# Rotary score products over all 128 rows instead of 64, with the upper rows zeroed by GpSimd

## The chip, the cores and the metric

The kernel runs on one core of a Trainium2 chip. The metric is the time of one execution on the device in microseconds (us), and the time of a kernel is the median of its runs. Five engines share the core: TensorE (PE in the profile, its weight loads PEld), VectorE (DVE), ScalarE (ACT), GpSimd (POOL) and SyncE (SP). Each runs its own list of instructions in order, and they wait for one another on semaphores.

## The reference

The reference is a stack of four layers for 256 tokens of width 2048: two of one family, then two (`l` = 0, 1) of another. The change lies in the latent attention of the last two. Each of 8 heads has queries and keys of 192 numbers: 128 plain ones, and 64 that are turned by the position (the rotary part). Scores are the dot product of all 192, so they are the sum of a product over 128 and one over 64.

```python
def mla_mixer(q_a, kv_a, k_rope, cos, sin, q_a_norm_g, w_q_b, kv_a_norm_g, w_kv_b, q_norm_g, k_norm_g):
    ...
    k_pe = jnp.broadcast_to(k_rope[:, :, None, :], (bsz, seq, MLA_HEADS, MLA_ROPE))
    k = jnp.concatenate([k_nope, k_pe], axis=-1)
    q = rms_norm(q, q_norm_g)
    k = rms_norm(k, k_norm_g)
    q = jnp.concatenate([q[..., :MLA_NOPE], apply_rope(q[..., MLA_NOPE:], cos, sin)], axis=-1)
    k = jnp.concatenate([k[..., :MLA_NOPE], apply_rope(k[..., MLA_NOPE:], cos, sin)], axis=-1)
    o = causal_block_attention(q, k, v, MLA_QK_HEAD ** -0.5)

def causal_block_attention(q, k, v, scale):
    for blk in range(seq // Q_BLOCK):            # Q_BLOCK = 128, so two blocks
        q0 = blk * Q_BLOCK
        kend = q0 + Q_BLOCK
        s = jnp.einsum('bqhd,bkhd->bhqk', q[:, q0:kend], k[:, :kend]).astype(jnp.float32) * scale
        mask = (q0 + jnp.arange(Q_BLOCK))[:, None] >= jnp.arange(kend)[None, :]
        p = jax.nn.softmax(jnp.where(mask, s, -jnp.inf), axis=-1)
        outs.append(jnp.einsum('bhqk,bkhd->bqhd', p.astype(v.dtype), v[:, :kend]))
```

The attention's output goes, beside that of a state-space mixer, through a projection (`w_out`), and the layer goes on with a cross attention and a feed-forward part.

## The kernel before

Nearly all the time goes into large products with weights. The weights come from memory in pieces of 128 x 2048 numbers. SP issues the transfers; ACT splits a piece into a high part (`w_hi`, L451, which waits until TensorE has done with the piece three earlier, `SETS = 3`); DVE computes the low part (`w_lo`, L459); and TensorE multiplies high by high, low by high and high by low (L531 to L533, L539 to L541, L547 and L549).

The small work of a layer, attention among it, is hung between these pieces. `layer_at(eng, l, idx, step)` puts a step on an engine's list behind piece `idx` of the layer. Each engine builds its list in the order of the pieces, so what stands in a list is fixed when the program is written, and only the semaphores decide when it runs.

The attention of layer `l` has eleven steps on TensorE, `step(0)` to `step(10)`, behind the pieces 34 to 44. In step `s` stand

- `load(s)`: eight transposes of head `s` (L1359 and L1360) into the scratch banks `M`; the last adds one to `la_turned`. ACT copies the 128 plain rows to `la["qk"]`, and DVE copies the 64 rotary rows to the lower half of `la["qkr"]` (L2199). There are two such buffers of 128 partitions x 512 numbers, for even and odd heads.
- `att_scores_pe` of head `s - 1`: for each of the two blocks of queries the plain product (L1030), the rotary product (L1032) and an addition of the causal mask as a product with the identity in bf16 (L1034). The first block takes 128 keys, the second 256. An fp32 product is two instructions in the profile.
- the product with the values of head `s - 3` (L1101, L1103) and the turn of head `s - 2`'s probabilities (L1088).

The maximum, the exponential and the scaling of a head's scores run on DVE (L1042, L1046, L1062, L1065) and ACT (L1055) meanwhile, and the turn in the next step waits for them.

GpSimd has little to do. Its list issues the small transfers. Around the change these are the gains of layer `l` (`mla_gains`), issued when the layer's first piece has started, and then, once both halves of the state-space output are ready (`ssd_out` at 2l + 2), the two parts of the transposed memory (`memT`) for the cross attention. The upper halves of `la["qkr"]` lie where temporaries of the rotation stood earlier (`la["rt"]`).

Of the kernel before, what the change touches and what calls it, by code (L numbers as in the profile page):

```python
# [28 lines left out]
P = 128  # L29
D = 2048  # L30
T = 256
# [102 lines left out]
def build(nc, dram, out_ap):  # L134
    ctx = ExitStack()
    with ctx:
# [5 lines left out]
        def S(name):  # L142
            if name not in sems:
                sems[name] = ctx.enter_context(nc.semaphore(name))
            return sems[name]
# [117 lines left out]
        la = dict(kr=Area(2048)(2, 8, 64), q=a(2, 8, 192), k=a(2, 8, P), v=a(2, 8, P))  # L263
# [517 lines left out]
        def n(eng, name, k=1):  # L781

            key = (eng.engine, name)
            tallies[key] = tallies.get(key, 0) + k
            return tallies[key]
# [238 lines left out]
        def att_scores_pe(pe, h, q, k, causal, rope=None):  # L1024
            pe.wait_ge(S("q_k_ready"), n(pe, "q_k_ready"))
            bank = M[:, 2 + h % 2, :]
            for t, (c0, w) in enumerate(cuts(causal)):
                tok = slice(t * P, t * P + P)
                o = bank[:, c0:c0 + w]
                mm = pe.matmul(o, q(h)[:, tok], k(h)[:, 0:w], start=(t == 0), stop=not causal, skip_group_check=True)  # L1030
                if rope:
                    pe.matmul(o, rope(h)[0][:, tok], rope(h)[1][:, 0:w], start=False, stop=False, skip_group_check=True)  # L1032
                if causal:
                    mm = pe.matmul(bank[:, c0 + w - P:c0 + w], identb[:, :], mask_ts[:, :], start=False, stop=True,  # L1034
                                   skip_group_check=True)
            mm.then_inc(S("att_scores"), 1)
# [48 lines left out]
        def att_turn_pe(pe, h, p, causal, l):  # L1085
            pe.wait_ge(S("att_probs"), n(pe, "att_probs"))
            for _, _, c, ct in blocks(causal):
                mm = pe.transpose(turn_bank(h, causal, l)[:, ct:ct + P], p[h % 2][:, c:c + P], ident[:, :])  # L1088
            mm.then_inc(S("att_turned"), 1)
# [6 lines left out]
        def att_values_pe(pe, h, pt, v, causal, l):  # L1096
            pe.wait_ge(S("att_pt"), n(pe, "att_pt"))
            if causal and h:
                pe.wait_ge(S("att_out"), n(pe, "att_out"))
            o = value_bank(h, causal, l)[:, 0:T]  # L1100
            pe.matmul(o, v(h, 0), pt[h % 2][:, 0:T], start=True, stop=False, skip_group_check=True)  # L1101
            if causal:
                mm = pe.matmul(o[:, P:T], v(h, 1), pt[h % 2][:, T:T + P], start=False, stop=True, skip_group_check=True)  # L1103
            else:
                mm = pe.matmul(o, v(h, 1), pt[h % 2][:, T:2 * T], start=False, stop=True, skip_group_check=True)
            mm.then_inc(S("att_values"), 1)
# [10 lines left out]
        def att_close_pe(pe, m):  # L1117

            pe.wait_ge(S("att_out"), n(pe, "att_out", m))
# [136 lines left out]
        def layer_at(eng, l, idx, step):  # L1256

            at_piece(eng, first_piece[f"ssd{l}"] + idx, step)
# [93 lines left out]
        def mla_pe(pe, l):  # L1352
            def load(h):
                if h:
                    pe.wait_ge(S("la_loaded"), n(pe, "la_loaded", 2))
                for j, (a, r) in enumerate(((la["q"][:, :, :, 0:P], la["q"][:, :, :, P:192]), (la["k"], la["kr"]))):
                    for t in range(NT):
                        c = j * T + t * P
                        pe.transpose(M[:, 0, c:c + P], a[:, t, h, :], ident[:, :])  # L1359
                        mm = pe.transpose(M[0:64, 1, c:c + P], r[:, t, h, :], ident[:, :])  # L1360
                mm.then_inc(S("la_turned"), 1)

            q = lambda h: la["qk"][h % 2][:, 0:T]
            k = lambda h: la["qk"][h % 2][:, T:2 * T]
            rope = lambda h: (la["qkr"][h % 2][0:64, 0:T], la["qkr"][h % 2][0:64, T:2 * T])
            v = lambda h, s: la["v"][:, s, h, :]

            def step(s):
                if s == 0:
                    pe.wait_ge(S("la_ready"), l + 1)  # L1370
                    pe.wait_ge(S("la_k"), l + 1)
                    pe.wait_ge(S("sd_exp"), 16 * l + 16)
                if s < 8:
                    load(s)
                if 0 <= s - 1 < 8:
                    if s - 1 < 2:
                        pe.wait_ge(S("z_root"), 2 * l + s)
                    att_scores_pe(pe, s - 1, q, k, True, rope)
                if 0 <= s - 3 < 8:
                    att_values_pe(pe, s - 3, la["pt"], v, True, l)  # L1380
                if 0 <= s - 2 < 8:
                    if s == 2:
                        c = plans[f"va{l}"][1]
                        pe.wait_ge(S(f"set_free{c.slot}"), c.c // 2 + 1)
                    att_turn_pe(pe, s - 2, la["p"], True, l)

            def close():
                att_close_pe(pe, 1)
                pe.wait_ge(S("la_loaded"), n(pe, "la_loaded", 2))

            for s in range(11):
                layer_at(pe, l, 34 + s, lambda s=s: step(s))
            layer_at(pe, l, 46, close)
# [887 lines left out]
        @block.sync  # L2281
        def _(sp):
            sp_stream(sp)
# [5 lines left out]
        @block.gpsimd  # L2289
        def _(pool):  # L2290

            def load(o, i, s):
                pool.dma_start(o, i).then_inc(S(s), 16)

            load(par[:], dram["params"], "first_const")
            load(ident[:], dram["ident"], "first_const")
            for o, nm in ((identb, "identb"), (mask_st, "mask_st"),
                          (mask_ts, "mask_ts"), (select, "head_select"), (level, "level"), (invf, "inv_freq"), (posi, "positions")):
                load(o[:], dram[nm], "const")
            load(cbias[:, 0:8], dram["c_b_i"][0].partition_broadcast(P), "const")  # L2300
            load(cbias[:, 8:16], dram["c_b_f"][0].partition_broadcast(P), "const")
            for v, nm in ((dt_b, "dt_bias_2"), (al_b, "a_log_2")):
                load(v, dram[nm].partition_broadcast(P), "const")
            load(ple_in[:], dram["pT"][0].rearrange("(k p) t -> p k t", p=P), "p_loaded")

            pool.wait_ge(S("piece_done"), started("lru", 3))
            for g, nm in enumerate(("b_w_r", "b_w_i")):
                load(lr["w"][:, g], dram[nm][0].rearrange("n c d -> c n d"), "gate_w")

            pool.wait_ge(S("lru_lo"), 1)  # L2310
            load(res[:], dram["x"].rearrange("b (t p) d -> p (b t) d", p=P), "res_back")

            pool.wait_ge(S("piece_done"), started("e_out_a", 1))
            load(pe_["gain"], dram["ple_norm"][0].partition_broadcast(P), "gain_loaded")
            load(mem_tokens, dram["mem_2"].rearrange("b (t p) d -> p (b t) d", p=P), "mem_tokens")
            load(ple_in[:], dram["pT"][1].rearrange("(k p) t -> p k t", p=P), "p_loaded")

            pool.wait_ge(S("piece_done"), started("o_out", 3))
            load(pe_["gain"], dram["ple_norm"][1].partition_broadcast(P), "gain_loaded")
            load(fin["gain"], dram["final_norm"].partition_broadcast(P), "final_gain")  # L2320
            for l in range(2):
                pool.wait_ge(S("piece_done"), started(f"ssd{l}"))
                load(mlag[:, 0, :], dram["mla_q_norm_g_2"][l].partition_broadcast(P), "mla_gain")
                load(mlag[:, 1, :], dram["mla_k_norm_g_2"][l].partition_broadcast(P), "mla_gain")

                pool.wait_ge(S("ssd_out"), 2 * l + 2)
                for j in range(2):
                    load(mem_parts[j], dram["memT"][:, 8 * j:8 * j + 8, :], "mem_loaded")
            for j, c in enumerate(plans["down12"]):
                pool.wait_ge(S(f"set_free{c.c % 2}"), c.c // 2 + 1)  # L2330
                cols = slice(512 * j, 512 * j + 512)
                pool.dma_start(out_ap[:, :, cols].rearrange("b (t p) d -> p (b t) d", p=P), res[:, :, cols]
                               ).then_inc(S("stored"), 16)
            pool.wait_ge(S("stored"), 64)
# [352 lines left out]
```

## Time and profile before

| | us |
|---|---|
| median of 3 runs | 3562.82 |
| lowest and highest run | 3557.84, 3564.38 |
| profiled execution, its own time | 3560.18 |
| its span, first to last instruction | 3558.4 |
| TensorE busy | 3479.6 |
| VectorE busy | 2106.5 |
| ScalarE busy | 1720.2 |
| GpSimd busy | 20.8 |

The span is 1.8 us shorter than the execution's own time; the rest lies before the first and behind the last instruction. A row that begins with a time is a place in the span. "Busy" of TensorE counts an instruction from its start to its modelled end, and these intervals overlap, so what a product really takes is read from the distance between two starts. In a form such as `64*128 64x256` the first pair is rows and columns of the array in use, the second the operand.

### The profile page before, as it was taken

To read this page: it belongs to the slowest core of one execution; us is meant where nothing else is said; L and a number is where in the kernel's file an instruction comes from. 1 tells how busy PE (TensorE), PEld (TensorE's weight loads), DVE (VectorE), ACT (ScalarE), POOL (GpSimd) and SP (SyncE) were. 2 spreads that over 40 slices of the span, in tenths; PEclk is the share of its full clock that TensorE was granted. 3 is DMA by queue.
4 is the path that set the end of the run, shared out by engine and by line. 5 is a ranking of instruction groups with operands and counts; after the bars stand their busy time and mean duration, and the time that the engine had idled before them with its cause. 6 is when DMAs were issued, how large, how long until landed. Compare 5 with 4: busy or idle time off the path is not lost.

```text
span 3558.4 us, 43532 instructions
## 1 busy us (share of the span) xinstructions
PE 3479.6 (98%) x18590; PEld 2974.1 (84%) x18590; DVE 2106.5 (59%) x2186; ACT 1720.2 (48%) x2040; POOL 20.8 (1%) x38
## 2 busy tenths in 40 slices
PE   7999999999999999999999999999999999999999
PEld 6888888878778888888888888888888888888887
DVE  6766667544556866646555545577656555455454
ACT  4643464356545465555434434455745644344343
POOL 1000000000000000000000000000000000000000
PEclk9999999999999999999999999999999999999999
DMA  6554554544555444445555555554444455555554
GB/s 241 185 178 142 192 190 167 195 171 170 187 176 180 173 142 154 146 147 181 189 189 190 189 192 190 191 181 166 142 141 168 149 189 190 194 189 189 189 189 166
DMA packets 88578, 630.91 MB, mean 177 GB/s; under 512 B 10064, under 2 KB 10304, under 8 KB 13248
## 3 DMA queue, kind: packets, MB, share of 16 engines
q1 hardware_dynamic: 85104, 611.75, 49.5%
q0 software_dynamic: 3280, 16.36, 1.3%
q8 instruction: 147, 2.41, 0.3%
q14 instruction: 47, 0.39, 0.0%
HBM read 625.98 MB, written 2.10 MB: 177 GB/s over the span
## 4 chain that ended last, share of the span: by engine, by line
PE 86%; DVE 7%; ACT 5%; issue 1%; DMA 1%; DVEq 0%; POOL 0%; ACTq 0%; POOLq 0%
PE G L547 26%; PE G L539 13%; PE G L549 13%; PE G L541 13%; PE G L540 13%; DVE w_lo L459 3%; ACT w_hi L451 2%; PE G L531 1%; PE G L533 1%; PE G L532 1%; PE M L811 1%; PE M L1139 1%; DMA w_raw<-in_s_lru 1%; DVE arena L758 0%; PE M L1032 0%
## 5 line engine op out<-in xcount | busy, mean ns | idle before, releaser
L459 DVE TENSOR_TENSOR w_lo<-w_raw,w_hi 128x2048 fp32r<-128x2048 f32 (+1 forms) x585 | 1328.3, 2272 | 1253.5 <-ACT w_hi L451 1253.1
L451 ACT ACTIVATE w_hi<-w_raw 128x2048 fp32r<-128x2048 f32 (+1 forms) x585 | 1110.8, 1899 | 1608.3 <-PE G L549 744.6
L547 PE MATMUL G<-x_halves,w_hi 128*128 128x512 f32 x4256 | 1346.3, 397 | 20.5 <-DVE w_lo L459 15.4
L549 PEld LDWEIGHTS G<-x_halves,w_lo 128*128 128x128 f32 x4256 | 800.9, 188 | 188.5
L549 PE MATMUL G<-x_halves,w_lo 128*128 128x256 f32 x4256 | 841.2, 278 | 0.0
L547 PEld LDWEIGHTS G<-x_halves,w_hi 128*128 128x128 f32 x4256 | 651.6, 189 | 24.9 <-issue 14.7
L539 PE MATMUL G<-w_hi,y_halves 128*128 128x512 f32 x1648 | 648.8, 394 | 3.0 <-DVE y_halves L1114 2.6
L541 PE MATMUL G<-w_hi,y_halves 128*128 128x512 f32 x1648 | 642.1, 390 | 0.0
L540 PE MATMUL G<-w_lo,y_halves 128*128 128x512 f32 x1648 | 642.0, 390 | 0.0
L539 PEld LDWEIGHTS G<-w_hi,y_halves 128*128 128x128 f32 x1648 | 309.7, 188 | 67.9 <-DVE y_halves L1114 4.4
L541 PEld LDWEIGHTS G<-w_hi,y_halves 128*128 128x128 f32 x1648 | 309.6, 188 | 65.3
L540 PEld LDWEIGHTS G<-w_lo,y_halves 128*128 128x128 f32 x1648 | 309.8, 188 | 62.6
L539 PE MATMUL G<-w_hi,x_halves 128*128 128x512 f32 x448 | 176.7, 394 | 0.0
L541 PE MATMUL G<-w_hi,x_halves 128*128 128x512 f32 x448 | 175.1, 391 | 0.0
L540 PE MATMUL G<-w_lo,x_halves 128*128 128x512 f32 x448 | 175.1, 391 | 0.0
L547 PE MATMUL G<-y_halves,w_hi 128*128 128x512 f32 (+1 forms) x400 | 127.1, 398 | 0.0
L681 DVE TENSOR_TENSOR arena<-G,other_half 128x512 f32<-128x512 f32 (+1 forms) x143 | 97.2, 679 | 9.9 <-ACT other_half L604 9.3
L541 PEld LDWEIGHTS G<-w_hi,x_halves 128*128 128x128 f32 x448 | 84.5, 189 | 17.9
L539 PEld LDWEIGHTS G<-w_hi,x_halves 128*128 128x128 f32 x448 | 84.6, 189 | 17.0
L540 PEld LDWEIGHTS G<-w_lo,x_halves 128*128 128x128 f32 x448 | 84.5, 189 | 17.0
L549 PEld LDWEIGHTS G<-y_halves,w_lo 128*128 128x128 f32 (+1 forms) x400 | 73.6, 184 | 17.4
L604 ACT ACTIVATE other_half<-G 128x512 f32<-128x512 f32 (+1 forms) x147 | 84.5, 575 | 1.2 <-ACT ple_in L1668 0.8
(442 smaller groups left out, 2703.9 us busy)
## 6 DMA issues: line engine op xcount, KB each, us to landing
w_raw<-in_s_up SPq DMA_DIRECT2D x176, 1024.0 KB, 4.8
w_raw<-in_s_down SPq DMA_DIRECT2D x88, 1024.0 KB, 4.8
w_raw<-in_s_ssd SPq DMA_DIRECT2D x40, 1024.0 KB, 4.8
w_raw<-in_s_hgrn SPq DMA_DIRECT2D x32, 1024.0 KB, 4.8
w_raw<-in_s_gate SPq DMA_DIRECT2D x32, 1024.0 KB, 4.8
w_raw<-in_s_mlstm SPq DMA_DIRECT2D x32, 1024.0 KB, 4.8
w_raw<-in_s_mlstm_gate SPq DMA_DIRECT2D x32, 1024.0 KB, 4.8
w_raw<-in_s_lru SPq DMA_DIRECT2D x16, 1024.0 KB, 4.9
```

Of the source, the lines that this page charges most:

```text
L451: act.activation(whi[p % SETS][:, 0:n_], raw[p % RAW][:, 0:n_], ACT.Copy).then_inc(S("hi_ready"), 1)
L459: dve.tensor_tensor(wlo[p % SETS][:, 0:n_], raw[p % RAW][:, 0:n_], whi[p % SETS][:, 0:n_].bitcast(F32), ALU.subtract).then_inc(S("lo_ready ...
L531: pe.matmul(o, ah[:, kk, tok], hi[:, k, :], start=first and t == 0, stop=False, **kw)
L532: pe.matmul(o, ah[:, kk, tok], lo[:, k, :], start=False, stop=False, **kw)
L533: mm = pe.matmul(o, al[:, kk, tok], hi[:, k, :], start=False, stop=last, **kw)
L539: pe.matmul(o, ah[:, kk, tok], hi[:, k, :], start=first, stop=False)
L540: pe.matmul(o, ah[:, kk, tok], lo[:, k, :], start=False, stop=False)
L541: mm = pe.matmul(o, al[:, kk, tok], hi[:, k, :], start=False, stop=last)
L547: pe.matmul(o, hi[:, k, f], x2, start=first, stop=False, skip_group_check=True)
L549: mm = pe.matmul(o[:, 0:T], lo[:, k, f], x2[:, 0:T], start=False, stop=last, skip_group_check=True)
L604: act.activation(other_half[0:np_, 0:nb, :], bank_set(c)[0:np_, 0:nb, T:2 * T], ACT.Copy).then_inc(S("half_out"), 1)
L681: dve.tensor_tensor(dst, bank_set(c)[0:np_, 0:nb, 0:T], other_half[0:np_, 0:nb, :], ALU.add).then_inc(S(f"set_free{c.c % 2}"), 1)
```

## The change

Both operands of the rotary product are now read over all 128 partitions instead of the lower 64. To make the added rows add nothing, GpSimd writes zeros to the partitions 64 to 127 of both buffers, once in each layer. It waits for the first head's transposes of that layer (`la_turned` at 8l + 1), and TensorE waits for it (`rope_padded`) in step 1, ahead of the first scores.

```diff
-            rope = lambda h: (la["qkr"][h % 2][0:64, 0:T], la["qkr"][h % 2][0:64, T:2 * T])
+            rope = lambda h: (la["qkr"][h % 2][:, 0:T], la["qkr"][h % 2][:, T:2 * T])
...
                 if s < 8:
                     load(s)
+                if s == 1:
+                    pe.wait_ge(S("rope_padded"), l + 1)
                 if 0 <= s - 1 < 8:
...
                 load(mlag[:, 1, :], dram["mla_k_norm_g_2"][l].partition_broadcast(P), "mla_gain")
+
+                pool.wait_ge(S("la_turned"), 8 * l + 1)
+                for v in la["qkr"]:
+                    ins = pool.memset(v[64:P, :], 0.0)
+                ins.then_inc(S("rope_padded"), 1)
 
                 pool.wait_ge(S("ssd_out"), 2 * l + 2)
```

On GpSimd, in the part of its list for one layer, there stood before the change these rows, where the two transfers of `memT` follow the gains directly:

```order
28 L2293 DMA mla_gains<-in_mla_q_norm_g 128x192 [waits piece_done]
29 L2293 DMA mla_gains<-in_mla_k_norm_g 128x192
30 L2293 DMA arena<-in_memT 128x2048 [waits ssd_out]
31 L2293 DMA arena<-in_memT 128x2048
32 L2293 DMA mla_gains<-in_mla_q_norm_g 128x192 [waits piece_done]
```

Now two memsets of `la["qkr"]` (part of the `arena`) stand between them:

```order
28 L2295 DMA mla_gains<-in_mla_q_norm_g 128x192 [waits piece_done]
29 L2295 DMA mla_gains<-in_mla_k_norm_g 128x192
30 L2330 MEMSET arena 64x512 [waits la_turned]
31 L2330 MEMSET arena 64x512
32 L2295 DMA arena<-in_memT 128x2048 [waits ssd_out]
33 L2295 DMA arena<-in_memT 128x2048
```

So the transfers of `memT` have the memsets and their wait ahead of them. On TensorE no instruction moves. In step 1 of a layer, at the first head's scores, its list reads now as follows (`ident` is the identity, `identb` the one in bf16, `mask_ts` the causal mask, `M` the scratch banks):

```order
5025 L1359 MATMUL M<-ident,arena 128x128
5026 L1360 MATMUL M<-ident,arena 64x128
5027 L1030 MATMUL M<-arena 128x128 [waits q_k_ready,z_root,rope_padded]
5028 L1032 MATMUL M<-arena 128x128
5029 L1034 MATMUL M<-mask_ts,identb 128x128
5030 L1030 MATMUL M<-arena 128x256
5031 L1032 MATMUL M<-arena 128x256
5032 L1034 MATMUL M<-mask_ts,identb 128x128
5033 L531 MATMUL G<-w_hi,y_halves 128x256 [waits ssd_out,lo_ready,set_free1]
```

The rows are the same as before but for `rope_padded` in the third. These lists show the size of the output, so they don't show the 64 or 128 rows that L1032 reads.

## Rows read from the trace of the kernel before

**Rows 1.** The page: busy time of TensorE, and shares of the chain that ended last.
```profile
PE 3479.6 (98%) x18590; PEld 2974.1 (84%) x18590; DVE 2106.5 (59%) x2186; ACT 1720.2 (48%) x2040; POOL 20.8 (1%) x38
...
PE 86%; DVE 7%; ACT 5%; issue 1%; DMA 1%; DVEq 0%; POOL 0%; ACTq 0%; POOLq 0%
```
**Rows 2.** Windows, busy us of each engine, granted clock, DMA: attention of both layers.
```profile
1378.00:1457.00 79.00, 79.00 (x569) 71.30 (x568) 45.82 (x87) 36.06 (x73) 0.41 (x1) 0.98 0.38 137
2588.00:2667.00 79.00, 79.00 (x575) 71.31 (x574) 45.80 (x87) 36.43 (x73) 0.81 (x2) 0.99 0.39 136
```
**Rows 3.** Timeline of PE, one head's scores: start, us, engine, line, operation.
```profile
1413.21 0.39 PE L1030 MATMUL M<-arena 128*128 128x128 f32 x2
1413.53 0.48 PE L1032 MATMUL M<-arena 64*128 64x128 f32 x2
1413.94 0.23 PE L1034 MATMUL M<-mask_ts,identb 128*128 128x128 bf16 x1
1414.01 0.65 PE L1030 MATMUL M<-arena 128*128 128x256 f32 x2
1414.59 0.70 PE L1032 MATMUL M<-arena 64*128 64x256 f32 x2
1415.22 0.23 PE L1034 MATMUL M<-mask_ts,identb 128*128 128x128 bf16 x1
```
**Rows 4.** Line L1032 in the whole program: weight loads, ns min/median/max, first and last.
```profile
L1032 PEld LDWEIGHTS M<-arena x64: 182/184/186, 1371.7 to 2653.2; 64*128 64x128 f32 x64
```
**Rows 5.** Timeline of PE: products over 128 and over 80 rows elsewhere.
```profile
1256.90 0.38 PE L1314 MATMUL M<-arena 128*128 128x128 f32 x2
1257.12 0.60 PE L1313 MATMUL M<-arena 128*128 128x256 f32 x2
1257.55 0.38 PE L1314 MATMUL M<-arena 128*128 128x128 f32 x2
1257.77 0.27 PE L1191 MATMUL M<-arena,head_select 80*128 80x256 bf16 x1
```
**Rows 6.** Timeline of PEld beside rows 3, then beside rows 5.
```profile
1414.59 0.29 PEld L1032 LDWEIGHTS M<-arena 64*128 64x128 f32 x2 [0.33 <-issue]
...
1257.34 0.41 PEld L1314 LDWEIGHTS M<-arena 128*128 128x128 f32 x2
```
**Rows 7.** Timeline of PE: last transpose of head 0; restart behind its scores.
```profile
1362.57 0.27 PE L1360 MATMUL M<-ident,arena 128*64 128x128 f32 x1
...
1371.37 0.39 PE L1030 MATMUL M<-arena 128*128 128x128 f32 x2
...
1376.48 0.39 PE L531 MATMUL G<-w_hi,y_halves 128*128 128x256 f32 x1 [2.87 <-ACT arena L649]
```
**Rows 8.** Timeline of DVE between these.
```profile
1362.92 0.69 DVE L689 TENSOR_TENSOR arena<-arena,rstd_row 128x512 f32<-128x512 f32 x1
1364.30 0.69 DVE L2101 TENSOR_TENSOR arena<-arena 128x512 f32<-128x512 f32 x1 [0.70 <-ACT arena L1621]
1367.50 2.29 DVE L459 TENSOR_TENSOR w_lo<-w_raw,w_hi 128x2048 fp32r<-128x2048 f32 x1 [2.50 <-ACT w_hi L451]
```
**Rows 9.** Groups of memsets by line: count, busy us, mean ns.
```profile
L1806 DVE MEMSET arena<- 128x3072 f32 x1 | 2.6, 2618 | 0.6 <-issue 0.6
L2677 POOL MEMSET const-float32-0.0<- 128x1 f32 x1 | 0.1, 94 | 0.2 <-issue 0.2
```
**Rows 10.** Timeline of POOL: the transfers of `memT` in layer 0.
```profile
1377.35 1.06 POOL L2293 DMA_DIRECT2D arena<-in_memT  x2 [240.03 <-DVE y_halves L2114]
```
**Rows 11.** Timelines of DVE and ACT: probabilities of a head; then the stage's end.
```profile
1410.20 0.55 DVE L1065 TENSOR_SCALAR diag<-diag,small 128x128 f32<-128x128 f32 x2
...
1457.20 1.91 ACT L451 ACTIVATE w_hi<-w_raw 128x2048 fp32r<-128x2048 f32 x1 [3.96 <-PE G L541]
```
**Rows 12.** Timeline of PE: the turn that reads these probabilities.
```profile
1415.99 0.27 PE L1088 MATMUL G<-ident,diag 128*128 128x128 f32 x1
```
**Rows 13.** Windows, columns as in rows 2: the stretch behind the restart.
```profile
1376.00:1386.00 10.00, 9.52 (x63) 9.03 (x63) 6.21 (x13) 7.83 (x12) 1.06 (x2) 0.83 0.74 287
```

## The prediction, as it was put on record before the changed kernel ran

> **What bounds the kernel now.** I began with the page. TensorE is busy for 98% of the span and holds 86% of the chain that ended last [rows 1], so time taken off TensorE counts wherever TensorE does not wait. Whether it waits where the change acts is read from the windows. In the attention of layer 0, from 1378 to 1457, TensorE is busy for 79.00 of 79 us and DVE for 45.8; in layer 1, from 2588 to 2667, it is the same [rows 2]. There the pace is TensorE's own. Then I read the timeline of one head's scores for the distance between starts [rows 3], set it against like products over 128 rows [rows 5], and looked at the weight loads beside both [rows 4, 6]. Last came the stretch around the first head of a layer, where the new memsets and the new wait lie [rows 7, 8].
>
> **What a rotary product costs now.** The starts of one head's products stand in [rows 3]. Plain pair over 128 keys: 1413.21 to 1413.53, 0.32 us. Rotary pair: to 1413.94, 0.41. Mask: 0.07. Second block, 256 keys: plain 0.58, rotary 0.63, mask again 0.07. Together 2.08 us. Pairs of the same size elsewhere, fp32 over 128 rows, take 1256.90 to 1257.12 = 0.22 us for 128 columns and 1257.12 to 1257.55 = 0.43 us for 256 [rows 5]. So a rotary pair takes 0.19 and 0.20 more than its columns ask for, and the plain pair ahead of it 0.10 and 0.15 more.
>
> The weight loads show where this goes. Over 128 rows a load begins while the products before it still run: the pair of L1314 loads at 1257.34 and multiplies at 1257.55 [rows 5, 6]. The second pair over 64 rows loads only at 1414.59, the time at which it multiplies, and behind 0.33 us in which the loader was idle [rows 3, 6]. A load over 64 rows is not taken ahead, and the product before it runs out first; the mask's load, back at 128 rows, waits in the same way. I read it as a price of each change between 64 and 128 rows: about 0.10 us to let the array run out on the way in, 0.10 for the first rotary load that nothing covers, and 0.10 on the way back.
>
> The row count is what sets the rotary pair apart. It isn't the operand: L1313 and L1314 change operands too, without a gap. Nor is it a partly filled array: L1191 uses 80 rows, and the fp32 pair before it still takes 0.22 us, as beside a full one [rows 5]. The trace has no other product over 64 rows or fewer to compare with.
>
> By one rule of the Trainium skill the change would bring nothing here. TensorE: Matmul & The Clock Gate, section "LDWEIGHTS (loading the stationary operand)", says that a load takes time by its columns and the row count doesn't matter. For the load itself the trace agrees (184 ns at 64 rows [rows 4]). But it is about one load's length and not about when it may begin; TensorEngine Tiling (Array Packing), section "Key Properties", says that a change of tiling mode drains the engine, which is what the idle loader looks like. By the first rule alone the time stays at 3560.2 to 3562.8; by the second the sum below holds.
>
> **The sum.** With 128 rows I take the rotary pairs at 0.22 and 0.43 (gains of 0.19 and 0.20), the first plain pair at 0.22 (gain 0.10), and the second at 0.48: its excess of 0.15 is 0.10 for the change of rows and 0.05 for a load behind the short mask product, which stays. That is 0.19 + 0.20 + 0.10 + 0.10 = 0.59 us a head; rounding of the starts leaves 0.57 to 0.60, and I take 0.58. A head's scores go from 2.08 to 1.50.
>
> There are 8 heads in 2 layers, 16 in all. The first head of each layer gains nothing: behind its scores TensorE waits until 1376.48 for ACT, 2.87 us [rows 7], and 0.58 less in front only lengthens that wait. That chain runs through DVE and ACT and holds none of these scores. The other 7 heads of a layer lie where TensorE never waits [rows 2]. 14 x 0.58 = 8.1 us.
>
> What could be late next? A head's probabilities are done at about 1410.8 and their turn comes at 1415.99 [rows 11, 12], 5.2 us later; steps that are 0.6 us shorter don't use that up, since the lag isn't added from step to step. At the stage's end ACT starts its split at 1457.20, released by TensorE [rows 11], so it comes earlier with it. I cost this at nothing; if the cover were gone, the loss could only be the 0.58 of a step.
>
> **The memsets and their wait.** The trace has none of this size on GpSimd. From below: its 128x1 memset, 94 ns. The nearest large one is DVE's 128x3072, 2618 ns [rows 9], which is 0.85 ns an element and 0.44 us for 512. From above I take the longest DVE instruction of the stretch, 2.29 us [rows 8], since GpSimd may be several times slower an element. I take 0.5 each, near DVE's, so 1.0 us a layer. They begin when head 0 is turned, at about 1362.9, and TensorE asks for them at 1371.37 [rows 7]: 8.5 us for 1.0, or 4.6 at the upper bound. Nothing, then. The transfers of `memT`, which now stand behind them, are issued at 1377.35 [rows 10], also later than 1367.5. The added semaphore on TensorE is asked once a layer, ahead of the wait to 1376.48, so it costs nothing. Below nothing there is no gain to be had: GpSimd released nobody here.
>
> What is not hidden is DVE. L689 starts at 1362.92 and L2101 at 1364.30 [rows 8], and this chain ends in TensorE's restart. If a memset holds DVE up, each layer's restart is late by as much: 0 to 1.0 us at my price, 0 to 4.6 at the upper bound. I take 0, as no DVE instruction of the trace has a GpSimd one beside it to say otherwise.
>
> On this the Trainium skill has two rules. GPSIMD Engine Reference, section "Key points", says that GpSimd contends with DVE instructions that have two SBUF inputs, as L689 has; by it the sum would be 1.0 us a layer less, 6.1. SBUF — State Buffer, section "Who interferes with whom", limits this to GpSimd instructions that read SBUF, which a memset doesn't; by it the sum stays at 8.1. No row of before shows either.
>
> The sum is made against the profiled execution's own time: 3560.18 - 8.1 = 3552.1. That execution lies 2.6 below the median of the runs; from the median it is 3562.8 - 8.1 = 3554.7. I forecast the middle, 3553.5.
>
> **The clock.** Behind the first head's wait the granted clock in 1376 to 1386 is 0.83 on the mean [rows 13]: 3.4 of the 10 us at the lower level, 1.2 GHz, which costs 1.7 us against 2.4 GHz. Before it fell TensorE had stood still for 2.87 us. The first head's scores now end 0.58 earlier, so the engine stands still for 3.5 us, and later idle times fall elsewhere. One more or one fewer such stretch is 1.7 us either way; I count no net change and widen the range by it.
>
> **The rivals.**
> - *Half the gain* (0.15). Only part is a matter of rows: the rotary loads go ahead, but the gaps stay, or the other way round. Half of 8.1 is 4.0: 3557.5. For it: the idle time, the uncovered load and the way back are three things in these rows. Against: all begin at the 64-row product, and none is seen at 128 or 80.
> - *No gain* (0.08). The row count doesn't matter, and the gap comes from something else about L1032, or the other engines take the time back. Time 3560.2 to 3562.8. Against it: [rows 5], and the 5.2 us of slack.
> - *GpSimd holds DVE up* (0.07). At 1.0 us a layer: 3555.5. It ends slower than before if two memsets stop DVE for more than 8.1 / 2 = 4.05 us a layer, so over 2.0 us each. At 2.29 each it is 9.2 - 8.1 = +1.1: 3563.9 from the median. For it: DVE is on the chain there. Against: 2 us is four times DVE's price, and 2.5 us in front of L459 are idle on DVE [rows 8].
> - *The wait is late* (0.02). The pair would have to take over 8.5 us, and then over the 2.87 of the wait behind it, before any is lost.
>
> **How the numbers follow.** The full gain holds 0.68. Its own range is 3550 to 3557: 1.7 for one clock stretch and some 2 for the spread of the runs (3557.8 to 3564.4). The range reaches up over the half and most of the none: 3549.0 to 3561.0. What a measurement can tell from no change is about 0.2%, or 7.1 us: below 3555.7. The full gain of 8.1 is only 1.0 beyond that, so I give it 0.75 to pass; the half and the held-up DVE pass in 1 of 6. 0.68 x 0.75 + 0.22 x 0.17 = 0.55 for faster. Slower by 0.2% needs over 11 us lost from the forecast's side: 0.03. The same: 0.42.
>
> **What would show it.** In the profile after, a head's scores take 1.50 us from L1030 to what follows (2.08 would refute it), the weight loads of L1032 start about 0.1 to 0.2 us before their products, and no 0.33 us of idle time stands before L1032 and L1034. TensorE's wait behind head 0 is 3.4 us instead of 2.87. The memsets take 0.5 us each and end before 1365; L689 keeps its 0.69 us and its start. Attention from the restart to the wait at its end is 7 x 0.58 = 4.1 us shorter in each layer. The forecast is wrong if this holds and the total moves by less than 5 us, for then a later wait took it, or if the pairs keep their gaps.

## The result, and the profile after

The changed kernel takes 3551.26 us (median of 8 runs, 3549.54 to 3553.63). The kernel before takes 3563.28 in 8 runs (3557.84 to 3570.28). The ratio is 0.9966 with a 95% interval of 0.9957 to 0.9974, so it is 9.3 to 15.3 us faster, 12.0 from median to median. The forecast was 3553.5.

The page of the changed kernel, the rows that answer to [rows 1]:

```profile
PE 3470.5 (98%) x18590; PEld 2975.9 (84%) x18590; DVE 2106.2 (59%) x2186; ACT 1719.6 (48%) x2040; POOL 22.7 (1%) x42
```

TensorE is busy for 9.1 us less with as many instructions, and GpSimd has four more, the memsets. The timeline of TensorE for the same head as in [rows 3]:

```profile
1410.80 0.39 PE L1030 MATMUL M<-arena 128*128 128x128 f32 x2
1411.03 0.39 PE L1032 MATMUL M<-arena 128*128 128x128 f32 x2
1411.25 0.22 PE L1034 MATMUL M<-mask_ts,identb 128*128 128x128 bf16 x1
1411.31 0.65 PE L1030 MATMUL M<-arena 128*128 128x256 f32 x2
1411.79 0.59 PE L1032 MATMUL M<-arena 128*128 128x256 f32 x2
1412.23 0.22 PE L1034 MATMUL M<-mask_ts,identb 128*128 128x128 bf16 x1
1412.28 0.43 PE L1101 MATMUL G<-level_masks,arena 128*128 128x256 f32 x1
```

From start to start: 0.23, 0.22, 0.06, 0.48, 0.44, 0.05, together 1.48 us where it was 2.08. It is the same for all 14 heads behind a layer's first: 1.477 us on the mean, from 2.076. Its weight loads are to be read against those of the kernel before. There, beside the second rotary load in [rows 6], stood the first one and the load of the mask behind:

```profile
1413.52 0.29 PEld L1032 LDWEIGHTS M<-arena 64*128 64x128 f32 x2
...
1415.21 0.10 PEld L1034 LDWEIGHTS M<-mask_ts,identb 128*128 128x128 bf16 x1 [0.33 <-issue]
```

In the changed kernel:

```profile
1410.92 0.30 PEld L1032 LDWEIGHTS M<-arena 128*128 128x128 f32 x2
...
1411.58 0.41 PEld L1032 LDWEIGHTS M<-arena 128*128 128x128 f32 x2
1412.01 0.10 PEld L1034 LDWEIGHTS M<-mask_ts,identb 128*128 128x128 bf16 x1
```

The rotary loads began with their products (1413.52 and 1413.53, 1414.59 and 1414.59); now they begin 0.11 and 0.21 us before them. The 0.33 us of idle time in front of the second one, and in front of the mask's load behind it, are gone. Behind the first head of the layer, as in [rows 7]:

```profile
1377.36 0.39 PE L531 MATMUL G<-w_hi,y_halves 128*128 128x256 f32 x1 [3.46 <-ACT arena L649]
```

The wait has grown from 2.87 to 3.46 us, by all that head 0's scores lost: no gain there. GpSimd in the same stretch, and DVE beside it, as in [rows 8, 10]:

```profile
1363.79 0.98 POOL L2330 MEMSET arena<- 64x512 f32 x2 [225.51 <-PE M L1360]
1378.24 1.06 POOL L2295 DMA_DIRECT2D arena<-in_memT  x2 [13.46 <-DVE y_halves L2116]
```

```profile
1363.80 0.69 DVE L689 TENSOR_TENSOR arena<-arena,rstd_row 128x512 f32<-128x512 f32 x1
1365.19 0.69 DVE L2103 TENSOR_TENSOR arena<-arena 128x512 f32<-128x512 f32 x1 [0.70 <-ACT arena L1623]
1368.39 2.29 DVE L459 TENSOR_TENSOR w_lo<-w_raw,w_hi 128x2048 fp32r<-128x2048 f32 x1 [2.50 <-ACT w_hi L451]
1370.60 0.68 DVE L2201 COPY arena<-M 64x512 f32<-64x512 f32 x1
```

The pair of memsets takes 0.98 us and ends at 1364.77, 7.5 us before TensorE starts head 0's scores at 1372.26. L689 runs wholly beside it and keeps its 0.69, and the distances to the next two DVE instructions (1.39 and 3.20) are those of before (1.38 and 3.20).

Timelines of PE, first of the kernel before and then of the changed one: TensorE's next wait at the end of each attention stage (L539), and the second layer's restart (L531):

```profile
1461.83 0.50 PE L539 MATMUL G<-w_hi,y_halves 128*128 128x512 f32 x1 [1.32 <-DVE y_halves L1114]
...
2586.86 0.58 PE L531 MATMUL G<-w_hi,y_halves 128*128 128x256 f32 x1 [2.87 <-ACT arena L649]
...
2671.98 0.50 PE L539 MATMUL G<-w_hi,y_halves 128*128 128x512 f32 x1 [1.32 <-DVE y_halves L1114]
```

```profile
1457.05 0.50 PE L539 MATMUL G<-w_hi,y_halves 128*128 128x512 f32 x1 [1.32 <-DVE y_halves L1114]
...
2581.86 0.58 PE L531 MATMUL G<-w_hi,y_halves 128*128 128x256 f32 x1 [3.46 <-ACT arena L649]
...
2664.01 0.50 PE L539 MATMUL G<-w_hi,y_halves 128*128 128x512 f32 x1 [1.32 <-DVE y_halves L1114]
```

From the restart to the wait at the stage's end the first layer took 85.35 us (from 1376.48 [rows 7]) and now takes 79.69, 5.7 less. The second took 85.12 and now takes 82.15, 3.0 less. Together that is 8.6, near the 8.4 = 14 x 0.60, but each by itself should be 4.2. The difference is the clock. The windows behind the restarts show it, the changed kernel first, then the one before (its first window is in [rows 13]; the last three columns are the granted clock, the DMA share and GB/s):

```profile
1376.00:1386.00 10.00, 8.64 (x70) 8.43 (x71) 6.83 (x14) 7.82 (x14) 1.06 (x2) 1.00 0.66 248
2576.00:2596.00 20.00, 16.54 (x114) 15.91 (x113) 12.99 (x20) 11.37 (x19) 1.07 (x2) 0.83 0.57 213
```

```profile
2576.00:2596.00 20.00, 16.31 (x99) 13.87 (x97) 12.69 (x18) 14.11 (x23) 1.07 (x2) 0.91 0.51 190
```

In the first layer the mean granted clock is 1.00 instead of 0.83, 1.7 us spared; in the second 0.83 instead of 0.91, 1.6 us more at half speed, some of it beside the wait. In this pair of traces they cancel. With half of the time at the lower clock taken off, the first stage goes from 83.64 to 79.68 us and the second from 83.68 to 79.32, 4.0 and 4.4 less.

The spans differ by 8.0 us (3558.4 and 3550.4), although the changed kernel came 0.9 us later to the restart of the first layer (1377.36 and 1376.48), and no instruction of TensorE differs up to the scores in front of it. The medians differ by 12.0. Two questions are left: whether the gap is a matter of the row change, and what the other 3.6 us are.

### The profile page after: what moved, and what is told of

Same layout as the page of the kernel before. It is cut to its first block, busy times and chain, and to the rows that moved or that the text cites. A ratio compares the mean times of both kernels' runs of the same rounds, so it can differ in the third digit from the quotient of the medians.

```text
span 3550.4 us, 43536 instructions
## 1 busy us (share of the span) xinstructions
PE 3470.5 (98%) x18590; PEld 2975.9 (84%) x18590; DVE 2106.2 (59%) x2186; ACT 1719.6 (48%) x2040; POOL 22.7 (1%) x42
## 4 chain that ended last, share of the span: by engine, by line
PE 86%; DVE 6%; ACT 5%; issue 1%; DMA 1%; DVEq 0%; POOL 0%; ACTq 0%; POOLq 0%
PE G L547 26%; PE G L539 13%; PE G L541 13%; PE G L549 13%; PE G L540 13%; DVE w_lo L459 3%; ACT w_hi L451 2%; PE G L531 1%; PE G L532 1%; PE G L533 1%; PE M L811 1%; DMA w_raw<-in_s_lru 1%; PE M L1139 1%; DVE arena L758 0%; PE M L1313 0%
## 5 line engine op out<-in xcount | busy, mean ns | idle before, releaser
L547 PE MATMUL G<-x_halves,w_hi 128*128 128x512 f32 x4256 | 1347.1, 398 | 20.1 <-DVE w_lo L459 15.3
L539 PE MATMUL G<-w_hi,y_halves 128*128 128x512 f32 x1648 | 648.9, 394 | 3.0 <-DVE y_halves L1114 2.6
L539 PEld LDWEIGHTS G<-w_hi,y_halves 128*128 128x128 f32 x1648 | 310.0, 188 | 68.3 <-DVE y_halves L1114 4.4
L539 PE MATMUL G<-w_hi,x_halves 128*128 128x512 f32 x448 | 176.9, 395 | 0.0
L539 PEld LDWEIGHTS G<-w_hi,x_halves 128*128 128x128 f32 x448 | 84.7, 189 | 17.0
```

The lines of the kernel that those rows point to most:

```text
L539: pe.matmul(o, ah[:, kk, tok], hi[:, k, :], start=first, stop=False)
L547: pe.matmul(o, hi[:, k, f], x2, start=first, stop=False, skip_group_check=True)
```

## The experiments

Each ratio is to the kernel before on the same chip, with its 95% interval. "Mean clock" is the mean over the runs of the granted clock that each run reports, to three decimals each.

**Is it the change between 64 and 128 rows?** Four runs change the products. The first, `grouped64`, is the kernel before with another order inside a head's scores (some arguments are left out here):

```diff
-            for t, (c0, w) in enumerate(cuts(causal)):
...
+            for t, tok, o, w in parts:
                 mm = pe.matmul(o, q(h)[:, tok], k(h)[:, 0:w], ...)
+            for t, tok, o, w in parts if rope else ():
+                pe.matmul(o, rope(h)[0][:, tok], rope(h)[1][:, 0:w], ...)
+            for t, tok, o, w in parts if causal else ():
+                mm = pe.matmul(o[:, w - P:w], identb[:, :], mask_ts[:, :], ...)
```

> The kernel before (64 rows, no memset), with the order inside a head's scores changed: both plain products, then both rotary ones, then both masks, so that the array changes between 128 and 64 rows once each way for a head instead of twice. Theory 'each change of rows costs': one way in and one way back (0.10 each) and one uncovered first load (0.10) go, 0.3 us of the 0.6 a head, and some 0.05 more for the masks side by side; scores about 1.72 us, 14 x 0.35 = 5 us shorter than before. Rival 'each 64-row product costs by itself' (its rows or its load are slow): the rotary pairs keep 0.41 and 0.63 us, scores at 2.02 or more, under 1 us shorter.

Measured: 3554.1, ratio 0.9977 (0.9967 to 0.9987), so 8.2 us shorter, where 5 were expected and the rival had under 1. Timelines of PE and of PEld, one head (L1029 is the plain product here, L1031 the rotary one, L1033 the mask):

```profile
1414.29 0.82 PE L1029 MATMUL M<-arena 128*128 128x128 f32 x4
1415.04 0.92 PE L1031 MATMUL M<-arena 64*128 64x128 f32 x4
...
1416.01 0.65 PE L1099 MATMUL G<-level_masks,arena 128*128 128x256 f32 x2
```

```profile
1415.04 0.52 PEld L1031 LDWEIGHTS M<-arena 64*128 64x128 f32 x4 [0.33 <-issue]
1415.89 0.11 PEld L1033 LDWEIGHTS M<-mask_ts,identb 128*128 128x128 bf16 x2 [0.33 <-issue]
```

1.72 us, as the first theory said. The four plain instructions take 0.75, 0.10 over their columns (0.22 and 0.43): the way in. The four rotary ones take 0.85: the same columns, one uncovered load and one way back. Between the two rotary pairs there is no gap, so a product over 64 rows does not cost by itself. Each way in and each way back does, once a head here. What the total has beyond the 5 us is taken up with the clock, below.

`grouped128` is the same edit on the changed kernel.

> The changed kernel with the same order inside a head's scores: plain, plain, rotary, rotary, mask, mask. Between 128-row products no change of rows is left, so only the load of 0.05 us behind the first mask can go: scores 1.42 instead of 1.48 us, 14 x 0.06 = 0.8 us shorter than the changed kernel, not distinguishable in the total. A rival by which the order itself matters beyond the rows would give as much here as in the 64-row kernel (0.3 us a head).

Measured: 3552.3, ratio 0.9969 (0.9957 to 0.9982), not distinguishable from the changed kernel. In the trace:

```profile
1413.42 0.82 PE L1029 MATMUL M<-arena 128*128 128x128 f32 x4
1414.08 0.82 PE L1031 MATMUL M<-arena 128*128 128x128 f32 x4
...
1414.84 0.43 PE L1099 MATMUL G<-level_masks,arena 128*128 128x256 f32 x1
```

1.42 us. The order alone is worth 0.05 us a head (1.477 to 1.424 on the mean); 0.30 of the 0.35 in `grouped64` were row changes saved. `rows96` and `rows32` change the row count:

```diff
-            rope = lambda h: (la["qkr"][h % 2][:, 0:T], la["qkr"][h % 2][:, T:2 * T])
+            rows = lambda h: 96
+            rope = lambda h: (la["qkr"][h % 2][0:rows(h), 0:T], la["qkr"][h % 2][0:rows(h), T:2 * T])
...
-                    ins = pool.memset(v[64:P, :], 0.0)
+                    ins = pool.memset(v[64:96, :], 0.0)
```

> The rotary products read 96 rows, and GpSimd zeroes the partitions 64 to 95 only. If the array is switched only at 64 rows or fewer, 96 behaves as 128: scores 1.48 us and loads taken ahead. If any row count other than that of the neighbours costs, the gaps are as at 64 rows: 2.08 us. The 80-row products of the trace speak for the first.

```diff
-            rope = lambda h: (la["qkr"][h % 2][0:64, 0:T], la["qkr"][h % 2][0:64, T:2 * T])
+            rows = lambda h: 32
+            rope = lambda h: (la["qkr"][h % 2][0:rows(h), 0:T], la["qkr"][h % 2][0:rows(h), T:2 * T])
```

> The kernel before with the rotary products over the lower 32 rows only (half of the rotary part is left out of the scores). If the gap belongs to any change to a part of the array, the steps are as at 64 rows: scores 2.08 us with the loads of L1032 uncovered. If a smaller part is switched in another way or costs by its rows, they differ.

Timelines of PE, `rows96` and then `rows32`:

```profile
1392.97 0.39 PE L1030 MATMUL M<-arena 128*128 128x128 f32 x2
1393.19 0.39 PE L1032 MATMUL M<-arena 96*128 96x128 f32 x2
...
1394.45 0.43 PE L1101 MATMUL G<-level_masks,arena 128*128 128x256 f32 x1
```

```profile
1387.51 0.39 PE L1030 MATMUL M<-arena 128*128 128x128 f32 x2
1387.83 0.48 PE L1032 MATMUL M<-arena 32*128 32x128 f32 x2
1388.24 0.23 PE L1034 MATMUL M<-mask_ts,identb 128*128 128x128 bf16 x1
...
1389.58 0.50 PE L1088 MATMUL G<-ident,ple_in 128*128 128x128 f32 x3
```

96 rows: 1.48 us, as 128. 32 rows: 2.07 us, as 64. So the gap sets in somewhere between 96 and 64 rows, and further down it costs the same. That 80 rows are free of it too rests on products in bf16, those of the kernel before that follow the last one in [rows 5]:

```profile
1257.89 0.22 PE L1192 MATMUL M<-arena,head_select 80*128 80x128 bf16 x1
1257.94 0.22 PE L1193 MATMUL M<-mask_st,identb 128*128 128x128 bf16 x1
```

The way from 80 rows back to 128 takes 0.05 us, and the next step between full products 0.06. Half the padding would do; GpSimd's memsets over 32 partitions took as long as over 64 (0.521 and 0.520 us).

It is the rows and not the columns of the array. The transposes of a head alternate between 128 and 64 columns, and the kernel before has no gap there, one product each 0.11 us:

```profile
1362.24 0.27 PE L1359 MATMUL M<-ident,arena 128*128 128x128 f32 x1
1362.35 0.27 PE L1360 MATMUL M<-ident,arena 128*64 128x128 f32 x1
```

**Which part of the change gains?** `pad_only` keeps the memsets and the wait, and reads 64 rows:

```diff
-            rope = lambda h: (la["qkr"][h % 2][:, 0:T], la["qkr"][h % 2][:, T:2 * T])
+            rope = lambda h: (la["qkr"][h % 2][0:64, 0:T], la["qkr"][h % 2][0:64, T:2 * T])
```

> GpSimd's memsets and TensorE's wait for them stay, but the rotary products read 64 rows as before. Theory A: within 2 us of the kernel before, a head's scores at 2.08 us, the memsets 0.52 us each and hidden. Theory B: the same, as TensorE's idle time behind head 0 is as before. Theory C: 3 to 4 us shorter than before.

Measured: 3564.43, ratio 0.9999 (0.9991 to 1.0008), scores 2.08 us. The letters A, B and C in these expectations are the theories that `after_again` names, below. Memsets and wait cost nothing and gain nothing, as far as the interval tells (some 3 us either way). Theory C falls. `first_head` and `other_heads` split the gain (one line `rows` each):

```diff
+            rows = lambda h: P if h == 0 else 64        # first_head
+            rows = lambda h: 64 if h == 0 else P        # other_heads
+            rope = lambda h: (la["qkr"][h % 2][0:rows(h), 0:T], la["qkr"][h % 2][0:rows(h), T:2 * T])
```

> Only head 0 of each layer uses 128 rows; heads 1 to 7 use 64 as before. Memsets and wait stay. Theory A: head 0's scores shrink by about 0.6 us and the wait behind them grows by as much (2.87 to about 3.45 us), so no gain: within 2 us of before. Theory B: the longer idle time there is what changes the clock, so 3 to 4 us shorter than before with a higher mean clock. Theory C: 3 to 4 shorter by the memsets.

> Heads 1 to 7 of each layer use 128 rows; head 0 uses 64 as before. Theory A: all of the gain, 14 x 0.60 = 8.4 us, the same time as the changed kernel within 2 us, and the wait behind head 0 back at 2.87 us. Theory B: 8.4 us shorter than before but 3 to 4 longer than the changed kernel. Theory C: as the changed kernel, 12 us shorter.

Measured: `first_head` 3562.54, ratio 0.9996 (0.9987 to 1.0005); `other_heads` 3552.52, ratio 0.9969 (0.9958 to 0.9980). The first is 1.4 us shorter than before, within its interval, and the second 11.0, within 2 us of the changed kernel: theory A holds in both. So the gain lies in heads 1 to 7, which is the 14 of the sum. In `other_heads` the wait is back at 2.88 us:

```profile
1376.07 0.39 PE L531 MATMUL G<-w_hi,y_halves 128*128 128x256 f32 x1 [2.88 <-ACT arena L649]
```

**Does GpSimd hold DVE up?** `long_memset` repeats the pair five times:

```diff
+                for i in range(4):
+                    for v in la["qkr"]:
+                        ins = pool.memset(v[64:P, :], 0.0)
+                    ins.then_inc(S("pad_again"), 1)
+                    pool.wait_ge(S("pad_again"), 4 * l + i + 1)
```

> The changed kernel with the two memsets repeated five times in a row in each layer, so that GpSimd is busy beside DVE for about 5 us (from 1363.8 on, about to 1369 or 1370) instead of 1.0, over L2101 and most of the split L459. Theory 'a memset does not hold DVE up': L2101 stays at 0.69 us, L459 at 2.29, the restart behind head 0 does not move. Rival 'GpSimd and DVE shut each other out': a DVE instruction there starts or ends up to 0.5 us late for each memset it meets, 1 to 3 us in all, and the restart is later by that. The wait of TensorE for the zeros is still hidden as long as they end before about 1372.

Timelines of POOL, of DVE and of TensorE's restart:

```profile
1365.48 4.11 POOL L2331 MEMSET arena<- 64x512 f32 x8 [225.49 <-PE M L1360]
1369.65 0.99 POOL L2335 MEMSET arena<- 64x512 f32 x2
```

```profile
1365.49 0.69 DVE L689 TENSOR_TENSOR arena<-arena,rstd_row 128x512 f32<-128x512 f32 x1
1366.88 0.69 DVE L2103 TENSOR_TENSOR arena<-arena 128x512 f32<-128x512 f32 x1 [0.70 <-ACT arena L1623]
1370.07 2.29 DVE L459 TENSOR_TENSOR w_lo<-w_raw,w_hi 128x2048 fp32r<-128x2048 f32 x1 [2.50 <-ACT w_hi L451]
```

```profile
1379.05 0.39 PE L531 MATMUL G<-w_hi,y_halves 128*128 128x256 f32 x1 [3.47 <-ACT arena L649]
```

Two DVE instructions lie wholly beside memsets and keep 0.69 us, and the split overlaps the last and keeps 2.29. From the start of L689 to the restart it is 13.56 us here, in the changed kernel and in the one before alike. No contention shows. `dve_zero` takes the other engine:

```diff
+                if s == 0:
+                    for v in la["qkr"]:
+                        ins = dve.memset(v[64:P, :], 0.0)
+                    ins.then_inc(S("rope_padded"), 1)
...
-                pool.wait_ge(S("la_turned"), 8 * l + 1)
-                for v in la["qkr"]:
-                    ins = pool.memset(v[64:P, :], 0.0)
-                ins.then_inc(S("rope_padded"), 1)
```

> The changed kernel, but VectorE writes the zeros (two memsets of 64x512 in step 0, ahead of its copy of the first head's rotary rows) and GpSimd does nothing for it. By VectorE's 0.85 ns an element each takes 0.44 to 0.5 us. They lie on the chain of VectorE and ScalarE that ends in TensorE's restart behind head 0: the restart is 0.9 us later in each layer, 1.8 us in all over the changed kernel, about 3553. A rival: VectorE is idle ahead of its split there, and the memsets fit in, so no loss.

Measured: 3556.35, ratio 0.9980 (0.9971 to 0.9988), some 5 us slower than the changed kernel by the ratios, whose intervals overlap (the changed kernel's is 0.9957 to 0.9974). 1.8 were expected. The timeline of DVE:

```profile
1367.92 2.29 DVE L459 TENSOR_TENSOR w_lo<-w_raw,w_hi 128x2048 fp32r<-128x2048 f32 x1 [2.50 <-ACT w_hi L451]
1370.38 1.03 DVE L2201 MEMSET arena<- 64x512 f32 x2 [0.16 <-issue]
1371.43 0.68 DVE L2205 COPY arena<-M 64x512 f32<-64x512 f32 x1
```

And TensorE's restart of the second layer:

```profile
2585.70 0.39 PE L531 MATMUL G<-w_hi,y_halves 128*128 128x256 f32 x1 [1.81 <-ACT arena L649]
```

From the start of the split to the copy it is 3.51 us instead of 2.21 in the changed kernel (1368.39 to 1370.60), so 1.3 us more and not 0.9: the pair takes 1.03, and the two small gaps around it the rest. All of it reaches TensorE's restart, which comes 14.87 us behind the start of L689 in both layers (1363.34 to 1378.21, 2570.83 to 2585.70), instead of 13.56. That is 2.6 of the 5 us. The mean clock is lower than the changed kernel's too (0.9932 and 0.9943, 3.9 us); the two together are more than the 5 measured, so the rest is not divided further. GpSimd is the right place for these zeros not by its speed, 0.52 us a memset where DVE takes 0.49, but because it is not on the chain.

**The other 3.6 us.** `after_again` repeats the changed kernel, `before_again` the one before, and `filled` fills the 0.60 us with a product over 128 rows:

```diff
+                if rope and t == 0:
+                    pe.matmul(bank[:, 0:352], q(h)[:, tok], la["qk"][h % 2][:, 0:352], start=True, stop=False,
+                              skip_group_check=True)
```

> The changed kernel once more, against the kernel before on the same chip. The two traces at hand show 0.60 us less for the scores of each of the 14 heads that lie on the path, 8.4 us in all, while the medians lie 12.0 apart. Theory A (only the gaps around the 64-row products): 8.4 us shorter in structure, with the rest from where the low-clock stretches fall in single executions, so the difference of medians comes out between 7 and 11. Theory B (the change also spares low-clock stretches as a rule): 11 to 14 again, and the mean granted clock of the changed kernel higher by about 0.001. Theory C (something else in the memsets or the wait gains): as B in time, with the same clock in both.

> The kernel before itself, as one of the compared kernels: no difference, a ratio whose interval holds 1, and a mean granted clock of 0.9925 to 0.9930 as in its 23 runs. If its clock here comes out near 0.994, the difference in clock between the kernels so far was chance.

> The changed kernel, with one product more in each head's scores: a plain product of 352 columns over 128 rows, overwritten by the first plain product, that fills the 0.60 us which the change saves. So the lengths between TensorE's waits are those of the kernel before, and no product reads 64 rows. Scores of a head: 1.48 + 0.60 = 2.07 us. So far the mean granted clock is 0.9927 over 23 runs of the kernel before and 0.9943 over 13 of the changed one, worth some 5 us beside the 8.4 of structure. Theory 'lengths': the clock depends on how long the stretches between waits are, so it falls back to about 0.9927 and the time to about 3563. Theory 'products': 64-row products lower the clock by themselves, so it stays at 0.994 and the time is about 3558 to 3559. Theory 'chance': 3560 to 3563 with a clock in between.

Measured: `after_again` 3550.44 us, 13.2 shorter than before by its ratio, with a mean clock of 0.9944. Both are what theory B named, a change that spares low clock as a rule, though the interval (8.2 to 17.8 us) does not exclude the 7 to 11 of theory A. `before_again` 3564.05, no difference, at 0.9928, so the clock of the kernel before repeats. `filled` 3561.14 at 0.9937, with scores of 2.07 us: what the theory of chance named.

| kernel | ratio (interval) | runs | mean clock | bare length of its trace, us |
|---|---|---|---|---|
| before, on three chips | 1 | 23, 14, 27 | 0.9927, 0.9928, 0.9928 | 3491.0 |
| before_again | 1.0001 (0.9993 to 1.0010) | 11 | 0.9928 | 3490.0 |
| pad_only | 0.9999 (0.9991 to 1.0008) | 11 | 0.9926 | 3491.1 |
| first_head | 0.9996 (0.9987 to 1.0005) | 11 | 0.9934 | 3491.9 |
| filled | 0.9995 (0.9986 to 1.0004) | 11 | 0.9937 | 3491.8 |
| changed | 0.9966 (0.9957 to 0.9974) | 8 | 0.9943 | 3482.6 |
| after_again | 0.9963 (0.9950 to 0.9977) | 5 | 0.9944 | 3483.4 |
| other_heads | 0.9969 (0.9958 to 0.9980) | 7 | 0.9934 | 3483.4 |
| rows32 | 3565.63 us | 1 | | 3489.5 |
| long_memset | 3553.13 us | 1 | | 3483.4 |
| rows96 | 3547.49 us | 1 | | 3483.3 |
| grouped64 | 0.9977 (0.9967 to 0.9987) | 9 | 0.9942 | 3486.5 |
| grouped128 | 0.9969 (0.9957 to 0.9982) | 6 | 0.9933 | 3484.2 |
| dve_zero | 0.9980 (0.9971 to 0.9988) | 11 | 0.9932 | 3484.2 |

The last column is worked out from each profiled execution: its span, less the time up to TensorE's 150th product, less half of the time after that, up to the last 30 us, in which its clock was at 1.2 GHz (37.5 us in the traces of both kernels, 47.8 in `before_again`, 23.9 in `rows96`). It is good to about 1 us, since a stretch at the lower clock can fall into a wait, where it costs less: in `dve_zero` the wait at the second restart is 1.81 us instead of 3.47. The first five rows, without the gain, come to 3491.2 on the mean (`rows32`, also without it, has 3489.5). The five with it, changed, `after_again`, `other_heads`, `long_memset` and `rows96`, come to 3483.2: 8.0 us less, against 14 x 0.60 = 8.4. `grouped64` has 4.7, against 14 x 0.35 = 4.9.

The attention stages show where these 8 us lie. From a layer's restart to the wait at the stage's end, again with half of the low-clock time taken off, it is 83.45 to 83.68 us in both layers of the six kernels without the gain, and 79.32 to 79.71 in those five with it: 4.1 us a layer on the mean.

What the medians have beyond it goes with the clock. 0.9927 to 0.9943 is 0.0016 of 3560 us, 5.7 us; each run's time multiplied by its own mean clock is on the mean 3537.6 over the 64 runs of before and 3530.9 over 13 runs of the changed kernel (`after_again` among them), 6.7 apart. So the structure gives 6.7 to 8.4 us of the 12, and 3.6 to 5.3 are a higher mean clock. Why it is higher is not settled. It is not simply the 64-row products: `filled` has none and its clock and time lie between the theories, and `dve_zero` has none and is at 0.9932. It isn't the memsets (`pad_only`, 0.9926), and head 0 alone (`first_head`, 0.9934) has less than half of the shift. The theory of lengths is not confirmed either, as `filled` did not come back to 0.9927. Against before, the clock is 0.0004 to 0.0017 higher in every kernel of the table with several runs except `before_again` and `pad_only`; no run tells luck of the distances between waits from a cause that would carry over.

## Why the prediction was right, point by point

- *What bounds it.* Right. TensorE never waited in these stages and does not now (busy for 74.00 of 74 us from 1379 to 1453); what it lost there came off the total.
- *The price of a change of rows.* Right in mechanism and nearly in size: 0.60 us a head, where 0.58 was taken. The missing 0.02 is the mask's two steps (0.056 us instead of 0.067 each), which I had left as they were. The rival of half the gain falls: loads and gaps went together, in both `rows96` and the changed kernel. I wrote that a load over 64 rows is not taken ahead; by `grouped64` that holds only behind a product over another number of rows.
- *The two rules.* The Trainium skill's page TensorEngine Tiling (Array Packing) says in section "Key Properties" that a change of tiling mode drains the engine, and lists 64 and 32 rows as modes, but not 96, in section "Available Configurations". The row counts measured here agree with it. It lists 128 rows by 64 columns too, and there the transposes above show no gap. The rule on the load's length (the Trainium skill, TensorE: Matmul & The Clock Gate, section "LDWEIGHTS (loading the stationary operand)") agrees too, 190 ns at 128 rows and 184 at 64, and says nothing on the gain.
- *14 of 16.* Right, by the wait of 3.46 us and by `first_head` and `other_heads`.
- *The memsets.* 0.52 us each for 0.5, hidden. The transfers of `memT` start 0.88 us behind TensorE's restart, as before (0.87).
- *GpSimd and DVE.* I took 0, and it is 0, also with ten memsets in a row. The limit that the Trainium skill's page SBUF — State Buffer, section "Who interferes with whom", puts on contention (only against a GpSimd instruction that reads SBUF) agrees; the wider sentence of its GPSIMD Engine Reference, section "Key points", by which the gain would be 6.1, does not hold for a memset.
- *The clock.* Mis-sized. I counted no net change and 1.7 us either way. Over all runs it gave 3.6 to 5.3 us, in the gain's favour. That is why 12.0 us came where 8.1 was summed. The sum itself measured 8.0 in the traces. That the forecast of 3553.5 lies only 2.2 us off is luck in part: the sum from the median of 3 runs gave 3554.7, and 3553.5 came from going halfway to one execution that lay 2.6 us below it.

## What to carry to other kernels

In a stream of fp32 products over 128 rows, one over 64 or fewer costs 0.3 us beyond its columns at each visit: look for weight loads that start with their own product behind an idle loader. Pad the operand on an idle engine to a row count without the gap (96 and 128 here), or put such products side by side. And where a change is worth a few us of TensorE's time, read the granted clock of every run before explaining the difference of medians.

## What the runs showed of the hardware

A memset of 64x512 fp32 took 0.52 us on GpSimd and 0.49 on DVE, and on GpSimd as long over 32 partitions. A product over 32 rows has the gaps of one over 64, one over 96 none, and a change between 128 and 64 columns has none either. The mean granted clock of one program differed between its executions: in 23 runs of the kernel before the slowest, 3566.9 us, had 0.991, and the fastest, 3560.1, had 0.994.
